# The end of a two-block layer kernel: last gate quarter in two halves, the mean per token earlier, one factor computed on GpSimd

## The chip, the core and the metric

The kernel runs on one core of a Trainium2 chip. The metric is the device time of one execution in microseconds. Three runs of the kernel before gave 1013.49 us as the median (1012.62 to 1014.14).

## The reference

The reference sends 256 tokens of width 1024 through two transformer blocks (four kinds of token mixers, a gated convolutional feed-forward part, a short-convolution layer, and a differential attention layer). All arithmetic is float32. Only its last lines matter here: the per-layer embedding of the second layer, which is added to x and is the output.

```
def per_layer_embed(x, p_i, g_pre, w_gate, w_proj, g_post):
    gate = jax.nn.sigmoid(rms_norm_2(x, g_pre) @ w_gate)
    return rms_norm_2(gate * (p_i @ w_proj), g_post)
...
x = x + per_layer_embed(x, p[i], g_pre_ple[i], w_ple_gate[i], w_ple_proj[i], g_post_ple[i])
```

So the end computes: x normed by its mean square per token, times a 1024 x 1024 weight (the gate), a sigmoid, the product with a projection that is ready by then, the mean square of that product per token, a norm by it, a gain, and the addition of x.

## The kernel before

All weights pass through one stream of blocks of 128 x 2048 elements. Each block is loaded by a DMA into a ring of three slots, ScalarE makes its rounded high part (`w_hi`, line 1639), VectorE the low part (`w_lo`, line 2433), and TensorE multiplies three times (high by high, high by low, low by high) and sums in PSUM. Each engine has its own list of instructions, written out by hand in the order in which they run; semaphores tie the lists together. An engine works strictly down its list, so whatever stands behind a waiting instruction waits too.

The activations are held channel-major (8 chunks of 128 channels x 256 tokens) nearly everywhere. The last gate (`ple_gate1`, four weight blocks, numbered 0 to 3, in function `last_layer` of TensorE) is computed token-major instead. Its result is 256 tokens x 1024 columns, cut in four quarters b = 0 to 3: quarter b holds token tile b // 2 (128 tokens) and column half b % 2 (512 columns). Before, quarter b is summed in PSUM bank `LAST_GATE_BANK[b]`, that is banks 6, 0, 1 and 2.

The sum of the last feed-forward layer (`y`) lies in PSUM banks 0 to 3 when the gate starts. VectorE scales it out of these banks in `add_before_gate` with five instructions, which raise the semaphore `y_scaled` five times: bank 0 in two halves (line 3114), then banks 1, 2 and 3 (line 3112). The list of VectorE has these five not in a row: behind bank 2 come two low parts of x chunks (line 2446), two updates of x (line 3118), one half weight block (line 3101), two more low parts, and only then bank 3. TensorE waits for the bank it is about to write: for the third scaling before quarter 2, for the fourth before quarter 3.

`mean_by_token` sums the squares of x over the channels for each token, with the result in PSUM bank 4. ScalarE turns this into r = (mean + eps)^-0.5 (`rstd_x`, lines 1720 and 1727), loads the sigmoid table (line 2230), and starts with `last_products`. There, for each quarter, ScalarE takes the sigmoid out of PSUM (line 2264), VectorE multiplies by the projection (line 3378) and by the gain (line 3382), and ScalarE squares and sums (line 2268). When the two quarters of a token tile are squared, VectorE turns the first sum into a bias (line 3386), ScalarE loads the table for logarithm and exponential (line 2287) and computes the factor as exp(-0.5 ln(...)) (lines 2276, 2277). The result is z times factor plus x. For that x is turned token-major on TensorE (`turn_x`, 16 transposes at line 885, into the banks `TURN_BANK` = 4, 5, 3, 7), and VectorE does the four additions (line 3394). Each raises a semaphore at which SyncE stores 256 KB (line 506).

The code at its places, with line numbers:

Of the kernel before, what the change touches and what calls it, by code (L numbers as in the profile page):

```python
# [16 lines left out]
P = 128  # L17
# [92 lines left out]
SUMS_OF_ROW = [3, 3, 4, 4, 3, 4, 4, 4]  # L110
LED = (3, 5, 6)
SIX_FIRST = (6, 0, 1, 2, 3, 4, 5, 7)
SQUARES_OF_POST = [5, 5, 3, 5, 5, 5]
SUMS_OF_POST = [2, 2, 0, 2, 2, 2]
# [3 lines left out]
TURN_BANK = (4, 5, 3, 7)  # L118
# [7 lines left out]
def build(nc, weights, small_in, x_in, masks_in, ident_in, channel_in, row_in, w_gk_in, p_in, table_in,  # L126
# [4 lines left out]
    with ExitStack() as ctx:  # L131
        sems = {}

        def sem(name):
            if name not in sems:
                sems[name] = ctx.enter_context(nc.semaphore(name))
            return sems[name]
# [304 lines left out]
        sum_of_squares, norm_bias, norm_r = (att_stat[0][:, a:b] for a, b in ((0, 4), (4, 6), (6, 8)))  # L442
# [108 lines left out]

# [3 lines left out]
        def _(pe):  # L555
# [246 lines left out]
            def last_layer(p, q):  # L802
# [27 lines left out]

                def part(j, b, k, a, w, first=False):

                    t, half = divmod(b, 2)
                    at = k % 2 * D + half * 512
                    return add(PS[:, LAST_GATE_BANK[b], :], a[:, k, t * P:(t + 1) * P], w[:, (n + j) % RING, at:at + 512], first)
# [13 lines left out]
                for b in (2, 3):  # L849
                    pe.wait_ge(sem("y_scaled"), T_PARTS * q + b + 1)  # L850
                    high(0, b, 0, True)
                    high(0, b, 1)
# [43 lines left out]
                gate(3, 0).then_inc(bank_summed, 1)  # L896
                gate(3, 1).then_inc(bank_summed, 1)
                mean_by_token()
                gate(3, 2).then_inc(bank_summed, 1)
                pe.wait_ge(sem("x_rstd"), p + 2)  # L900
                pe.wait_ge(sem("proj_copied"), 6)
                for b in range(4):
                    turn_x(b)
                gate(2, 3)
                gate(3, 3).then_inc(bank_summed, 1)
# [716 lines left out]
        def _(act):  # L1622
# [633 lines left out]
            def last_products(q):  # L2256
# [8 lines left out]

                def square(b):
                    act.wait_ge(sem("ple_product"), 5 + b + 1)
                    act.activation(sq4[:, b, :], by_quarter[:, b, :], ACT.Square, accum_out=sum_of_squares[:, b:b + 1]) \  # L2268
                        .then_inc(sem("y_squares"), 1)

                def rstd(t):

                    act.wait_ge(sem("y_squares"), y_square(q, 2 * t + 2))
                    act.wait_ge(sem("y_sum"), y_sum(q, t + 1))
                    r = norm_r[:, t:t + 1]
                    link(act.activation(r, sum_of_squares[:, 2 * t + 1:2 * t + 2], ACT.Ln, scale=1.0 / D, bias=norm_bias[:, t:t + 1]))
                    act.activation(r, r, ACT.Exp, scale=-0.5).then_inc(sem("y_rstd"), 1)
# [4 lines left out]
                square(0)  # L2282
                square(1)
                gate_sigmoid(2)
                square(2)
                gate_sigmoid(3)
                act.preload_act_table_set(TABLES)
                rstd(0)
                square(3)
                rstd(1)  # L2290
# [118 lines left out]
        def _(dve):  # L2409
# [961 lines left out]
            def last_products(z, q):  # L3371
# [7 lines left out]

                def gain(b):  # L3380
# [3 lines left out]
                def bias(t):  # L3384
                    dve.wait_ge(sem("y_squares"), y_square(q, 2 * t + 1))
                    ts(norm_bias[:, t:t + 1], sum_of_squares[:, 2 * t:2 * t + 1], 1.0 / D, EPS, ALU.mult, ALU.add) \
                        .then_inc(sem("y_sum"), 1)

                def result(b):
                    if b % 2 == 0:  # L3390
                        settle()
                        dve.wait_ge(sem("y_rstd"), q + b // 2 + 1)
                        dve.wait_ge(sem("mixed_turned"), 4 + 4)
# [290 lines left out]
```

## Time and profile before

| | |
|---|---|
| median of 3 runs | 1013.49 us |
| the profiled execution | 1012.54 us, of which the span of the profile is 1010.8 us |
| TensorE matmul busy | 996.4 us (99%), 8338 instructions |
| VectorE busy | 845.2 us (84%) |
| ScalarE busy | 622.3 us (62%) |
| GpSimd busy | 7.3 us (1%) |
| share of the chain that ended last | PE 93%, DVE 2%, ACT 2%, DMA 2% |

TensorE works nearly without a break from the start to about 1002 us of the span. Only the last 9 us belong to others: the last products on ScalarE and VectorE in turn, and the stores. In the last of the 40 slices of the page the busy share of PE is 6 tenths, and DVE and ACT show 6 tenths each. In the rows PE is TensorE, PEld its weight load, DVE VectorE, ACT ScalarE, POOL GpSimd, SP SyncE.

### The profile page before, as it was taken

To read this page: it belongs to the slowest core of one execution; us is meant where nothing else is said; L and a number is where in the kernel's file an instruction comes from. 1 tells how busy PE (TensorE), PEld (TensorE's weight loads), DVE (VectorE), ACT (ScalarE), POOL (GpSimd) and SP (SyncE) were. 2 spreads that over 40 slices of the span, in tenths; PEclk is the share of its full clock that TensorE was granted. 3 is DMA by queue.
4 is the path that set the end of the run, shared out by engine and by line. 5 is a ranking of instruction groups with operands and counts; after the bars stand their busy time and mean duration, and the time that the engine had idled before them with its cause. 6 is when DMAs were issued, how large, how long until landed. Compare 5 with 4: busy or idle time off the path is not lost.

```text
span 1010.8 us, 20806 instructions
## 1 busy us (share of the span) xinstructions
PE 996.4 (99%) x8338; PEld 934.7 (92%) x8338; DVE 845.2 (84%) x1216; ACT 622.3 (62%) x858; POOL 7.3 (1%) x18
## 2 busy tenths in 40 slices
PE   8999999999999999999999999999999999999996
PEld 7999999999999998899999999989999999999985
DVE  6974896899988878879998888889776899988886
ACT  6754565657565655467575646775677666565665
POOL 0000001000000000000000000000000000000000
PEclk9999999999999999999999999999999999999998
DMA  9533315555655545656556555535444356655531
GB/s 333 182 117 97 126 49 196 168 205 172 209 203 172 202 144 190 206 211 233 197 187 207 190 184 197 175 128 179 156 149 166 128 184 207 212 197 177 202 126 42
DMA packets 26786, 177.04 MB, mean 175 GB/s; under 512 B 3261, under 2 KB 3541, under 8 KB 6368
## 3 DMA queue, kind: packets, MB, share of 16 engines
q1 hardware_dynamic: 25616, 171.31, 48.9%
q0 software_dynamic: 1104, 4.78, 1.6%
q8 instruction: 50, 0.82, 0.4%
q14 instruction: 16, 0.13, 0.0%
HBM read 175.02 MB, written 2.63 MB: 176 GB/s over the span
## 4 chain that ended last, share of the span: by engine, by line
PE 93%; DVE 2%; ACT 2%; DMA 2%; issue 0%; SPq 0%; DVEq 0%
PE PS L606 80%; PE PS L557 12%; DMA arena<-masks_in 1%; DVE arena L2574 1%; DMA raw<-weights 0%; DVE w_lo L2433 0%; PE PS L1544 0%; ACT xn L2268 0%; ACT arena L1807 0%; ACT w_hi L1639 0%; ACT arena L2264 0%; PE PS L912 0%; ACT arena L2003 0%; ACT arena L1808 0%; DVE arena L2984 0%
## 5 line engine op out<-in xcount | busy, mean ns | idle before, releaser
L606 PE MATMUL PS<-h_store,w_hi 128*128 128x256 f32 (+1 forms) x1840 | 475.9, 338 | 2.0 <-DVE w_lo L2488 1.6
L2433 DVE TENSOR_TENSOR w_lo<-raw,w_hi 128x2048 fp32r<-128x2048 f32 x152 | 347.9, 2290 | 50.5 <-ACT w_hi L1639 45.4
L606 PE MATMUL PS<-h_store,w_lo 128*128 128x256 f32 (+1 forms) x1400 | 365.4, 281 | 0.1
L1639 ACT ACTIVATE w_hi<-raw 128x2048 fp32r<-128x2048 f32 x155 | 296.1, 1911 | 82.6 <-PE PS L606 69.5
L606 PEld LDWEIGHTS PS<-h_store,w_hi 128*128 128x128 f32 x1840 | 303.8, 187 | 41.3 <-DVE w_lo L2488 2.0
L606 PEld LDWEIGHTS PS<-h_store,w_lo 128*128 128x128 f32 (+1 forms) x1400 | 253.2, 188 | 0.5 <-DVE h_store L3047 0.3
L606 PE MATMUL PS<-act_hi,w_hi 128*128 128x256 f32 x688 | 191.0, 279 | 0.1
L606 PE MATMUL PS<-act_hi,w_lo 128*128 128x256 f32 x688 | 190.6, 279 | 0.1
L606 PE MATMUL PS<-act_lo,w_hi 128*128 128x256 f32 x688 | 187.5, 279 | 0.0
L606 PEld LDWEIGHTS PS<-act_hi,w_hi 128*128 128x128 f32 x688 | 129.3, 188 | 1.6 <-DVE act_hi L3047 0.6
L606 PEld LDWEIGHTS PS<-act_hi,w_lo 128*128 128x128 f32 x688 | 129.3, 188 | 0.3 <-DVE act_hi L3047 0.3
L606 PEld LDWEIGHTS PS<-act_lo,w_hi 128*128 128x128 f32 x688 | 127.4, 188 | 0.0
L2116 ACT ACTIVATE arena<-PS 128x512 f32<-128x512 f32 x51 | 30.2, 593 | 88.6 <-PE PS L606 88.6
L2108 ACT ACTIVATE arena<-arena,channel 128x256 f32<-128x256 f32 x132 | 63.6, 531 | 13.4 <-DVE arena L3187 12.2
L606 PE MATMUL PS<-w_hi,h_store 128*128 128x256 f32 (+1 forms) x352 | 70.6, 306 | 0.5 <-ACT h_store L1763 0.5
L3164 DVE SCALAR_TENSOR_TENSOR arena<-arena,channel 128x254 f32<-128x254 f32 x132 | 57.9, 480 | 7.6 <-DVE arena L3160 0.3
L3160 DVE SCALAR_TENSOR_TENSOR arena<-arena,channel 128x255 f32<-128x255 f32 x132 | 57.7, 479 | 0.9 <-ACT arena L2108 0.9
L606 PEld LDWEIGHTS PS<-w_hi,h_store 128*128 128x128 f32 x352 | 54.6, 188 | 3.9 <-ACT w_hi L1753 0.9
L3185 DVE TENSOR_TENSOR arena<-PS,arena 128x512 f32<-128x512 f32 x51 | 35.0, 686 | 21.1 <-ACT arena L2116 21.1
L606 PE MATMUL PS<-w_lo,h_store 128*128 128x256 f32 (+1 forms) x176 | 45.1, 302 | 0.5 <-DVE w_lo L2433 0.5
L557 PE MATMUL PS<-h_store,w_hi 128*128 128x256 f32 x256 | 45.4, 279 | 0.0
L557 PE MATMUL PS<-arena 64*64 64x64 f32 (+8 forms) x1356 | 41.5, 224 | 0.0
(385 smaller groups left out, 1138.1 us busy)
## 6 DMA issues: line engine op xcount, KB each, us to landing
raw<-weights SPq DMA_DIRECT2D x155, 1024.0 KB, 5.0
raw<-weights SPq DMA_DIRECT2D x12, 256.0 KB, 4.0
arena<-masks_in SPq DMA_DIRECT2D x1, 1600.0 KB, 12.2
bias_by_key<-bias_by_distance POOLq DMA_DIRECT2D x1, 1536.0 KB, 8.1
x<-x_in SPq DMA_DIRECT2D x4, 256.0 KB, 4.3
raw<-weights SPq DMA_DIRECT2D x2, 512.0 KB, 8.9
arena<-weights POOLq DMA_DIRECT2D x2, 512.0 KB, 6.0
arena<-bias_by_key POOLq DMA_DIRECT2D x1, 1024.0 KB, 6.4
```

Of the source, the lines that this page charges most:

```text
L557: return pe.matmul(o, lhs, rhs, start=start, stop=stop)
L606: return pe.matmul(o, lhs, rhs, start=start, stop=stop, skip_group_check=True)
L1639: act.activation(w_hi[:, slot, :], raw[:, slot, :], ACT.Copy).then_inc(hi_ready, 1)
L2108: ins = act.activation(dst[:, c, :], src[:, c, :], ACT.Identity, scale=w, bias=b)
L2116: act.activation(low, PS[:, bank:bank + 2, TOK:512], ACT.Copy).then_inc(sem("low_copied"), 1)
L2433: tt(w_lo[:, slot, :], raw[:, slot, :], w_hi[:, slot, :].bitcast(F), ALU.subtract).then_inc(lo_ready, 1)
L2574: mark(stt(dst, PS[:, bank_of_block(n), f * TOK:(f + 1) * TOK - d], ch("gdn_conv", (3 - d) * 6 + 2 * s + f), dst, ALU.mult, ALU.add))
L3160: stt(y[:, c, 1:TOK], src[:, c, 0:TOK - 1], channel[:, bass.ds(col(1) + c, 1)], y[:, c, 1:TOK], ALU.mult, ALU.add).then_inc(ready[0], 1)
L3164: ins = stt(y[:, c, 2:TOK], src[:, c, 0:TOK - 2], channel[:, bass.ds(col(0) + c, 1)], y[:, c, 2:TOK], ALU.mult, ALU.add)
L3185: tt(z, PS[:, bank:bank + 2, 0:TOK], low, ALU.add).then_inc(sem("parts_added"), 1)
```

## The change

Five things change, all in the last few dozen microseconds:

1. Quarter 3 of the gate is summed as two halves of 256 columns, the first in bank 2 and the second in bank 3. Every 512-column matmul of this quarter becomes two of 256 columns, and its last two blocks are now run half after half, at the very end. Before its first matmul TensorE waits for the fifth scaling as well, since bank 3 is now written.
2. `mean_by_token` stands behind quarter 0 of the last block, before it stood behind quarter 1.
3. The transposes of quarter 2 go to bank 6, before to bank 3. So they wait for the first sigmoid, which reads bank 6.
4. The factor of the first token tile is computed as a power on GpSimd, in place of the logarithm and exponential on ScalarE. Ahead of the power (line 553 of the changed file) the program has one more GpSimd instruction of the kind ISA on the same line, which has no operands and no wait. The sum of both squares and eps is formed by one VectorE instruction, and the squares carry the factor 1/1024 themselves.
5. The last square is done on VectorE as one multiply-and-sum of 256 columns; ScalarE squares the first half of quarter 3 only, and loads its table behind the last sigmoid as before. The first result is added before the last half products, the other three at the end.

The diff, cut to its core:

```diff
-SQUARES_OF_POST = [5, 5, 3, 5, 5, 5]
-SUMS_OF_POST = [2, 2, 0, 2, 2, 2]
+SQUARES_OF_POST = [5, 5, 3, 5, 5, 4]
+SUMS_OF_POST = [2, 2, 0, 2, 2, 3]
...
-TURN_BANK = (4, 5, 3, 7)
+TURN_BANK = (4, 5, 6, 7)
...
+            link(pool.memset(minus_half, -0.5))
+            pool.wait_ge(sem("y_sum"), y_sum(5, 1))
+            pool.tensor_tensor(norm_r[:, 0:1], norm_bias[:, 0:1], minus_half, ALU.pow).then_inc(sem("first_rate"), 1)
...
+                def last_quarter(j, k, half, a, w, first=False, final=False):
+
+                    at = k % 2 * D + 512 + half * TOK
+                    return add(PS[:, 2 + half, 0:TOK], a[:, k, P:TOK], w[:, (n + j) % RING, at:at + TOK], first, final)
+
                 def part(j, b, k, a, w, first=False):
 
+                    if b == 3:
+                        last_quarter(j, k, 0, a, w, first)
+                        return last_quarter(j, k, 1, a, w, first)
...
                 for b in (2, 3):
                     pe.wait_ge(sem("y_scaled"), T_PARTS * q + b + 1)
+                    if b == 3:
+                        pe.wait_ge(sem("y_scaled"), T_PARTS * q + 5)
                     high(0, b, 0, True)
                     high(0, b, 1)
...
                 gate(3, 0).then_inc(bank_summed, 1)
+                mean_by_token()
                 gate(3, 1).then_inc(bank_summed, 1)
-                mean_by_token()
                 gate(3, 2).then_inc(bank_summed, 1)
                 pe.wait_ge(sem("x_rstd"), p + 2)
                 pe.wait_ge(sem("proj_copied"), 6)
+                pe.wait_ge(sem("gate_sigmoid"), 5 + 1)
                 for b in range(4):
                     turn_x(b)
-                gate(2, 3)
-                gate(3, 3).then_inc(bank_summed, 1)
+                for half in range(2):
+                    for k in range(4, KC):
+                        last_quarter(k // 2, k, half, a_hi, w_hi)
+                        last_quarter(k // 2, k, half, a_lo, w_hi)
+                        last = last_quarter(k // 2, k, half, a_hi, w_lo, False, k == KC - 1)
+                    last.then_inc(bank_summed, 1)
...
                 gate_sigmoid(0)
                 gate_sigmoid(1)
                 square(0)
+                gate_sigmoid(2)
                 square(1)
-                gate_sigmoid(2)
                 square(2)
-                gate_sigmoid(3)
+                half_sigmoid(0)
+                act.wait_ge(sem("ple_product"), 5 + 4)
+                act.activation(sq4[:, 3, 0:TOK], prod[:, 6, :], ACT.Square, scale=D ** -0.5, accum_out=sum_of_squares[:, 3:4]) \
+                    .then_inc(sem("y_squares"), 1)
+                half_sigmoid(1)
                 act.preload_act_table_set(TABLES)
-                rstd(0)
-                square(3)
-                rstd(1)
+                act.wait_ge(sem("y_sum"), y_sum(q, 3))
+                r = norm_r[:, 1:2]
+                link(act.activation(r, sum_of_squares[:, 4:5], ACT.Ln, bias=norm_bias[:, 1:2]))
+                act.activation(r, r, ACT.Exp, scale=-0.5).then_inc(sem("y_rstd"), 1)
...
                 product(0)
                 product(1)
                 gain(0)
-                bias(0)
                 gain(1)
                 product(2)
+                mean(0, 0, 1, 2)
                 gain(2)
-                bias(1)
-                product(3)
-                gain(3)
-                for b in range(4):
-                    result(b)
+                half_product(0)
+                dve.wait_ge(sem("first_rate"), 1)
+                result(0)
+                half_gain(0)
+                half_product(1)
+                dve.wait_ge(sem("ple_product"), 5 + 5)
+                v = prod[:, 7, :]
+                dve.tensor_tensor_reduce(sq4[:, 3, TOK:512], v, v, 1.0 / D, 0.0, ALU.mult, ALU.add, sum_of_squares[:, 4:5]) \
+                    .then_inc(sem("y_sum"), 1)
+                mean(1, 2, 3, 4)
+                half_gain(1)
+                result(1)
+                dve.wait_ge(sem("y_rstd"), q + 1)
+                result(2)
+                result(3)
```

On TensorE, in the gate's first block (h_store holds the activations, w_hi and w_lo the weights), the rows from the last matmuls of quarter 2 over quarter 3 into the low parts were before:

```order
L606 MATMUL PS<-w_hi,h_store 128x512
L606 MATMUL PS<-w_lo,h_store 128x512
L606 MATMUL PS<-w_hi,h_store 128x512 [waits y_scaled]
L606 MATMUL PS<-w_lo,h_store 128x512
L606 MATMUL PS<-w_hi,h_store 128x512
L606 MATMUL PS<-w_lo,h_store 128x512
L606 MATMUL PS<-w_hi,h_store 128x512 [waits lo_chunk]
L606 MATMUL PS<-w_hi,h_store 128x512 x3
```

and are now:

```order
L608 MATMUL PS<-w_hi,h_store 128x512
L608 MATMUL PS<-w_lo,h_store 128x512
L608 MATMUL PS<-w_hi,h_store 128x256 [waits y_scaled]
L608 MATMUL PS<-w_hi,h_store 128x256
L608 MATMUL PS<-w_lo,h_store 128x256 x2
L608 MATMUL PS<-w_hi,h_store 128x256 x2
L608 MATMUL PS<-w_lo,h_store 128x256 x2
L608 MATMUL PS<-w_hi,h_store 128x512 [waits lo_chunk]
L608 MATMUL PS<-w_hi,h_store 128x512 x2
```

Quarter 3 is the group behind the last `waits y_scaled`. Its four wide matmuls are now eight narrow ones, and the count for which that wait holds is five scalings, before four.

On TensorE again, from quarter 1 of the last block to the transposes (`ones,arena` is the mean per token, `ident,x` the transposes), the rows were before:

```order
L606 MATMUL PS<-w_hi,h_store 128x512 x2
L606 MATMUL PS<-w_lo,h_store 128x512
L606 MATMUL PS<-w_hi,h_store 128x512 x2
L606 MATMUL PS<-w_lo,h_store 128x512
L606 MATMUL PS<-ones,arena 128x2 [waits x_sum]
L606 MATMUL PS<-ones,arena 128x2
L606 MATMUL PS<-w_hi,h_store 128x512 x2
L606 MATMUL PS<-w_lo,h_store 128x512
L606 MATMUL PS<-w_hi,h_store 128x512 x2
L606 MATMUL PS<-w_lo,h_store 128x512
L885 MATMUL PS<-ident,x 128x128 [waits proj_copied,x_rstd]
```

and are now:

```order
L608 MATMUL PS<-w_hi,h_store 128x512 x2
L608 MATMUL PS<-w_lo,h_store 128x512
L608 MATMUL PS<-ones,arena 128x2 [waits x_sum]
L608 MATMUL PS<-ones,arena 128x2
L608 MATMUL PS<-w_hi,h_store 128x512 x2
L608 MATMUL PS<-w_lo,h_store 128x512
L608 MATMUL PS<-w_hi,h_store 128x512 x2
L608 MATMUL PS<-w_lo,h_store 128x512
L608 MATMUL PS<-w_hi,h_store 128x512 x2
L608 MATMUL PS<-w_lo,h_store 128x512
L608 MATMUL PS<-w_hi,h_store 128x512 x2
L608 MATMUL PS<-w_lo,h_store 128x512
L897 MATMUL PS<-ident,x 128x128 [waits gate_sigmoid,proj_copied,x_rstd]
```

The mean stands six matmuls sooner, and the first transpose has a third wait.

On VectorE, the end of the list (products at line 3378, gains at 3382, results at 3394; the line numbers of the changed file are 3397 and 3401 for products, 3405 and 3409 for gains, 3420 for results) was before:

```order
L3386 TENSOR_SCALAR arena<-arena 128x1 [waits y_squares]
L3382 TENSOR_TENSOR arena<-arena 128x512 [waits ple_product]
L3378 TENSOR_TENSOR arena<-arena 128x512 [waits gate_sigmoid]
L3382 TENSOR_TENSOR arena<-arena 128x512 [waits ple_product]
L3386 TENSOR_SCALAR arena<-arena 128x1 [waits y_squares]
L3378 TENSOR_TENSOR arena<-arena 128x512 [waits gate_sigmoid]
L3382 TENSOR_TENSOR arena<-arena 128x512 [waits ple_product]
L3394 SCALAR_TENSOR_TENSOR arena<-arena,PS 128x512 [waits mixed_turned,y_rstd,dve_own]
L3394 SCALAR_TENSOR_TENSOR arena<-arena,PS 128x512
L3394 SCALAR_TENSOR_TENSOR arena<-arena,PS 128x512 [waits mixed_turned,y_rstd,dve_own]
L3394 SCALAR_TENSOR_TENSOR arena<-arena,PS 128x512
```

and is now:

```order
L3414 TENSOR_SCALAR arena<-arena 128x1 [waits y_squares]
L3405 TENSOR_TENSOR arena<-arena 128x512 [waits ple_product]
L3401 TENSOR_TENSOR arena<-arena 128x256 [waits gate_sigmoid]
L3420 SCALAR_TENSOR_TENSOR arena<-arena,PS 128x512 [waits mixed_turned,dve_own,first_rate]
L3409 TENSOR_TENSOR arena<-arena 128x256 [waits ple_product]
L3401 TENSOR_TENSOR arena<-arena 128x256 [waits gate_sigmoid]
L3439 ISA xn,arena<-arena 128x256 [waits ple_product]
L3439 ISA arena 128x1
L3414 TENSOR_SCALAR arena<-arena 128x1 [waits y_squares]
L3409 TENSOR_TENSOR arena<-arena 128x256 [waits ple_product]
L3420 SCALAR_TENSOR_TENSOR arena<-arena,PS 128x512 [waits mixed_turned,dve_own]
L3420 SCALAR_TENSOR_TENSOR arena<-arena,PS 128x512 [waits mixed_turned,dve_own,y_rstd]
```

One result now stands behind `first_rate`, GpSimd's semaphore, ahead of the last half product, and the multiply-and-sum (line 3439) stands between the last product and the second mean.

## Rows read from the trace of the kernel before

**Rows 1.** PE timeline, gate's first block; start us, us, engine line op, count.

```profile
977.91 0.47 PE L606 MATMUL PS<-w_hi,h_store 128*128 128x512 f32 x1 [0.53 <-ACT h_store L1763]
...
980.52 0.39 PE L606 MATMUL PS<-w_lo,h_store 128*128 128x512 f32 x1
980.75 0.39 PE L606 MATMUL PS<-w_hi,h_store 128*128 128x512 f32 x1
```

**Rows 2.** VectorE timeline of the same stretch.

```profile
978.00 1.28 DVE L3112 TENSOR_TENSOR arena<-PS,arena 128x512 f32<-128x512 f32 x2
...
980.78 1.22 DVE L3101 TENSOR_TENSOR w_lo<-raw,w_hi 128x1024 fp32r<-128x1024 f32 x1
...
982.71 0.68 DVE L3112 TENSOR_TENSOR arena<-PS,arena 128x512 f32<-128x512 f32 x1
```

**Rows 3.** chain that ended last, up to 996 us; start us, us, what.

```profile
977.78 0.14 issue
977.91 18.19 PE PS L606 x81
```

**Rows 4.** PE timeline from the mean per token to the end.

```profile
995.71 0.50 PE L606 MATMUL PS<-ones,arena 128*128 128x2 f32 x4
996.07 0.71 PE L606 MATMUL PS<-w_hi,h_store 128*128 128x512 f32 x2
...
997.53 1.91 PE L885 MATMUL PS<-ident,x 128*128 128x128 f32 x16
999.19 0.71 PE L606 MATMUL PS<-w_hi,h_store 128*128 128x512 f32 x2
...
1001.80 0.39 PE L606 MATMUL PS<-w_lo,h_store 128*128 128x512 f32 x1
```

**Rows 5.** ScalarE timeline of the end.

```profile
996.25 0.26 ACT L1720 ACTIVATE arena<-PS,eps 128x4 f32<-128x4 f32 x1 [6.25 <-PE PS L606]
...
998.06 1.27 ACT L2264 ACTIVATE arena<-PS,arena 128x512 f32<-128x512 f32 x2
999.61 0.63 ACT L2268 ACTIVATE xn<-arena 128x512 f32<-128x512 f32 x1 [0.28 <-DVE arena L3378]
...
1003.60 1.28 ACT L2287 ACT_TABLE_LOAD   x1
```

**Rows 6.** VectorE timeline of the end.

```profile
993.32 0.43 DVE L2465 TENSOR_TENSOR arena<-arena 128x256 f32<-128x256 f32 x1
998.88 1.29 DVE L3378 TENSOR_TENSOR arena<-arena 128x512 f32<-128x512 f32 x2 [5.13 <-ACT arena L2264]
...
1005.51 2.72 DVE L3394 SCALAR_TENSOR_TENSOR arena<-arena,PS 128x512 f32<-128x512 f32 x4 [0.48 <-ACT arena L2277]
```

**Rows 7.** chain that ended last, its last piece.

```profile
1007.57 0.66 DVE arena L3394
```

**Rows 8.** PE timeline, 256-column matmuls in steady run.

```profile
968.94 0.28 PE L606 MATMUL PS<-act_hi,w_hi 128*128 128x256 f32 x1
969.05 0.28 PE L606 MATMUL PS<-act_lo,w_hi 128*128 128x256 f32 x1
```

**Rows 9.** ScalarE timeline, one reading of 256 columns of PSUM.

```profile
969.62 0.36 ACT L1788 ACTIVATE xn<-PS 128x256 f32<-128x256 f32 x1
```

**Rows 10.** groups by form, VectorE; line, op, shapes, count, busy us, mean ns.

```profile
L3454 DVE CUSTOM_DVE_ANT_0 arena<-PS,arena 128x256 f32<-128x256 f32 x16 | 6.7, 420 | 0.0
...
L3454 DVE DVE_READ_ACCUMULATOR2_ANT arena<- 128x1 f32 x16 | 1.3, 83 | 0.0
```

**Rows 11.** groups on GpSimd, its largest memset.

```profile
L522 POOL MEMSET zeros_r<- 128x512 f32 x1 | 0.5, 530 | 0.0
```

**Rows 12.** windows; us, busy of PE, PEld, DVE, ACT, POOL, then PEclk.

```profile
1004.00:1005.00 1.00, 0.00 (x0) 0.00 (x0) 0.97 (x2) 0.99 (x2) 0.00 (x0) 0.89 0.00 0
1005.00:1006.00 1.00, 0.00 (x0) 0.00 (x0) 0.52 (x2) 0.97 (x4) 0.00 (x0) 0.50 0.00 0
```

**Rows 13.** groups by form, PE, first 7 us: the zero matmuls.

```profile
L606 PE MATMUL PS<-zeros_r 128*128 128x512 f32 x13 | 4.7, 531 | 1.5 <-POOL zeros_r L522 1.5
```

More of the change, by code:

```diff
@@ L109 @@
 }
-SUMS_OF_ROW = [3, 3, 4, 4, 3, 4, 4, 4]
+SUMS_OF_ROW = [3, 3, 4, 4, 3, 4, 4, 5]
 LED = (3, 5, 6)
 SIX_FIRST = (6, 0, 1, 2, 3, 4, 5, 7)
-SQUARES_OF_POST = [5, 5, 3, 5, 5, 5]
-SUMS_OF_POST = [2, 2, 0, 2, 2, 2]
+SQUARES_OF_POST = [5, 5, 3, 5, 5, 4]
+SUMS_OF_POST = [2, 2, 0, 2, 2, 3]
 POST_BANK = (5, 4, 4, 5, 4)
@@ L441, in build @@
         by_quarter = prod.rearrange("p c n -> p (c n)").rearrange("p (b n) -> p b n", b=4)
-        sum_of_squares, norm_bias, norm_r = (att_stat[0][:, a:b] for a, b in ((0, 4), (4, 6), (6, 8)))
+        sum_of_squares, norm_bias, norm_r, minus_half = (att_stat[0][:, a:b] for a, b in ((0, 5), (5, 7), (7, 9), (9, 10)))
         def hi_at(p, c):
@@ L2264, in gate_sigmoid, with half_sigmoid @@
                     act.activation(flat(z[b]), PS[:, LAST_GATE_BANK[b], :], ACT.Sigmoid, scale=r_x[:, at:at + 1]).then_inc(sem("gate_sigmoid"), 1)
+                def half_sigmoid(half):
+                    act.wait_ge(bank_summed, bank_sum(7, 4 + half))
+                    act.activation(z[3][:, half, :], PS[:, 2 + half, 0:TOK], ACT.Sigmoid, scale=r_x[:, TOK + 2:TOK + 3]) \
+                        .then_inc(sem("gate_sigmoid"), 1)
                 def square(b):
                     act.wait_ge(sem("ple_product"), 5 + b + 1)
-                    act.activation(sq4[:, b, :], by_quarter[:, b, :], ACT.Square, accum_out=sum_of_squares[:, b:b + 1]) \
+                    act.activation(sq4[:, b, :], by_quarter[:, b, :], ACT.Square, scale=D ** -0.5, accum_out=sum_of_squares[:, b:b + 1]) \
                         .then_inc(sem("y_squares"), 1)
[L2271 to L2277, printed above, removed]
                 act.wait_ge(sem("x_rstd"), 8)
@@ L3378, in product, with half_product @@
                     tt(by_quarter[:, b, :], quarter(z[b]), by_quarter[:, b, :], ALU.mult).then_inc(sem("ple_product"), 1)
+                def half_product(half):
+                    dve.wait_ge(sem("gate_sigmoid"), 5 + 4 + half)
+                    tt(prod[:, 6 + half, :], z[3][:, half, :], prod[:, 6 + half, :], ALU.mult).then_inc(sem("ple_product"), 1)
                 def gain(b):
@@ L3382, in gain, with half_gain, mean @@
                     mark(tt(quarter(z[b]), by_quarter[:, b, :], gain_row[:, (b % 2) * 512:(b % 2 + 1) * 512], ALU.mult))
[L3384 to L3387, printed above, removed]
+                def half_gain(half):
+                    dve.wait_ge(sem("ple_product"), 5 + 4 + half)
+                    mark(tt(z[3][:, half, :], prod[:, 6 + half, :], gain_row[:, 512 + half * TOK:512 + (half + 1) * TOK], ALU.mult))
+                def mean(t, first, second, squares):
+                    dve.wait_ge(sem("y_squares"), y_square(q, squares))
+                    ts(norm_bias[:, t:t + 1], sum_of_squares[:, first:first + 1], sum_of_squares[:, second:second + 1], EPS,
+                       ALU.add, ALU.add).then_inc(sem("y_sum"), 1)
                 def result(b):
[L3390 to L3393, printed above, removed]
+                    settle()
+                    dve.wait_ge(sem("mixed_turned"), 4 + 4)
                     stt(by_quarter[:, b, :], quarter(z[b]), norm_r[:, b // 2:b // 2 + 1], PS[:, TURN_BANK[b], :], ALU.mult, ALU.add) \
```

## The prediction

> **What bounds the kernel now.** I read the chain of waits first, then the timelines of TensorE, VectorE and ScalarE from 968 us on, then a few groups and the windows of the last microseconds. The chain has one piece of TensorE that starts at 977.91 us and runs 18.19 us through 81 matmuls [rows 3]: from the first matmul of the last gate to the mean per token TensorE never stops. So whatever holds TensorE up there moves the end by as much, and whatever is taken out in front of the mean comes off it. Behind the mean the chain goes to ScalarE and VectorE, which hand the quarters to each other: the reader is to see in the ScalarE and VectorE timelines that sigmoid, product, square and again product follow within 0.1 us of each other [rows 5, 6]. TensorE works beside them until its last matmul at 1001.80 [rows 4], and it is no longer what they wait for. The last addition on VectorE ends at 1008.23 (1007.57 plus 0.66) [rows 7], and the stores behind it, 2.6 us to the end of the span at 1010.8, are the same in both kernels.
>
> **The change part by part.**
>
> First, the new wait in the gate's first block. Quarter 3 starts there at 980.75 now [rows 1]; the two scalings of banks 1 and 2 began at 978.00 and took 1.28 us together, so the old wait was over at 979.28 [rows 2] and cost nothing. The changed kernel writes bank 3 as well, and must wait for the fifth scaling. On VectorE that is the single L3112 that starts at 982.71 and lasts 0.68, so it ends at 983.39 [rows 2]; between it and the fourth stand the half weight block of 1.22 us at 980.78 [rows 2] and seven smaller instructions, none of which waits for TensorE, so it comes no sooner. TensorE starts a matmul 0.14 us after its release [rows 3]: 983.53 in place of 980.75, that is 2.78 us of standing still. The first matmul after a wait lasts 0.47 us where the next ones last 0.39 [rows 1], which adds 0.08. Nothing gives this back: TensorE has no idle time from there to the mean [rows 3], and its in-order list holds all the rest of the gate behind the wait. ScalarE's high part of the last weight block, which waits for the first block to be used, slips with it, but it and VectorE's low part come some 2 us before they are wanted.
>
> Second, twelve matmuls of 512 columns in the first two blocks become 24 of 256. A steady 512-column matmul costs 0.226 us: from 996.07 to 997.53 there are 6 and some hundredths of start-up, and (1001.80 - 999.19)/11 is 0.237 with a start-up of 0.1 in it [rows 4]. A 256-column one costs 0.11 to 0.12 [rows 8]; I take 0.117. 24 times 0.117 less 12 times 0.226 is 0.10 us. Bounds: 0.11 would give -0.07, 0.12 gives +0.17. With the stall the shift is 2.78 + 0.08 + 0.10 = 2.96 us.
>
> Third, the mean stands 6 matmuls sooner: 6 times 0.226 = 1.36 us off. It starts at 995.71 now [rows 4], so at 995.71 + 2.96 - 1.36 = 997.31. It needs the sum of squares, whose last fold ends at 993.75 now [rows 6]. That fold stands behind work that the stall pushes by up to 2.5 us, which makes about 996.2, still a microsecond early.
>
> Fourth, the walk from the mean's start to the last addition, which takes 12.52 us now (995.71 to 1008.23). Taken from the start of the mean as zero: the first sigmoid starts at 2.35 (998.06) and the first product at 3.17 (998.88) [rows 5, 6], and the first square 0.73 after its product (999.61) [rows 5]. These steps are the same after. Then ScalarE: a square holds it for 0.63 [rows 5], so the third sigmoid, now ahead of the second square, starts at 4.53 and ends by 5.2. VectorE: products and gains of 512 columns follow each other at 0.61 (a pair takes 1.29, one 0.69 by the difference of ends) [rows 6]: second product 3.78, gains 4.39 and 5.00, third product 5.61, first mean 6.22, third gain 6.29. The third square follows the third product by 0.73 at 6.34 and ends at 6.97. The first half sigmoid reads 256 columns in 0.36 [rows 9], and its product starts at 7.38. Then the chain lies on VectorE: product half 0.35, first result at 7.73 with 0.66 (four results take 2.72) [rows 6], gain half 0.35 at 8.39, second half product at 8.74. Its sigmoid stands behind the half square (7.84) and is done by 8.7. The multiply-and-sum must see that product written, which makes 9.20; it takes 0.42 and 0.08 for its sum, by the 16 such instructions of 256 columns in the attention [rows 10]. Second mean 9.70, gain half 9.77, then the wait for that gain's write, and the results at 10.23, 10.89, 11.55, end at 12.29. ScalarE loads its table for 1.28 us [rows 5] from 8.54 to 9.82, and needs 0.5 more for logarithm and exponential, so the second factor is there at 10.35, before it is wanted at 10.89. This walk is 0.23 us shorter than now. Bounds: each of its eight hand-overs between engines or through a semaphore may be 0.05 off either way, so 0.2 less to 0.6 us more (a late hand-over adds, an early one is often covered by the other engine).
>
> The stretch of TensorE beside it is not in the way. The mean takes 0.36 (995.71 to 996.07), two quarters 2.71, so the transposes start at 3.1 from the mean, and the added wait, for the first sigmoid, ends at 3.05. The transposes take 1.66 us (997.53 to 999.19) [rows 4] and a half 12 times 0.117 = 1.4: the first half is summed at 6.5 against 6.97, when ScalarE comes to it, the second at 7.9 against 8.3. Without the split TensorE would finish at the same time, so the two halves buy only that the first can be read earlier.
>
> The power on GpSimd is new: no row shows one. It starts when the first mean is written, at 6.37, and its answer is wanted at 7.73, so it has 1.36 us. The nearest rows are a GpSimd memset of 512 columns at 0.53 us [rows 11] and, as an upper bound, ScalarE's load of a table together with such a memset, 1.81 us. I take 0.6, nearest to GpSimd's own row, and it is hidden; from 1.36 on every tenth counts in full, since VectorE stands at that wait with the last half product behind it. The upper bound gives +0.45.
>
> Sum: 2.96 - 1.36 - 0.23 = +1.37 us. The profiled execution took 1012.54 us, its span 1010.8; the span would be 1012.2 and that execution 1013.9. The median lies 0.95 above the profiled one, so I put the sum on the median: 1013.49 + 1.37, rounded to 1014.8 us. The change takes a quarter of a gate block out of the path and pays two of them for it at bank 3.
>
> **The rivals.**
>
> Rival A, TensorE's clock falls in the stall (slower). At the end of the run TensorE's last matmul starts at 1001.80 and ends at 1002.19 [rows 4], and the granted clock is at 0.89 in the window from 1004 and at 0.50 in the next [rows 12], so it fell at about 1004.8, 2.6 us after the last matmul. The new stall leaves TensorE without work for about as long: from 980.91 to 983.53 is 2.6 us. If the clock falls from 2.4 to 1.2 GHz there, the gate's matmuls go on at half pace until it rises. What that costs can be read from the start: the 13 matmuls on zeros take 4.7 us, mean 531 ns [rows 13], where 12 times 0.226 plus 0.39 would be 3.1. That is 1.6 us lost in one such rise, so 1014.8 + 1.6 = 1016.4 us, and 1018 if it lasts twice as long. Against it: the two times are only just alike, and TensorE was busy in front of the stall. The Trainium skill (TensorE: Matmul & The Clock Gate, Part 1) says that the gate is set by how busy TensorE has recently been and is not in step with the kernel's start; by that rule some executions would show this and others not, which no run here can tell yet.
>
> Rival B, GpSimd answers late. For it speaks the nameless extra instruction ahead of the power, against it that it stands ahead of the wait, so that it can be done long before the power is released. By the bound above 1014.8 + 0.45 = 1015.3 us. The Trainium skill (GPSIMD Engine Reference, 2.1 Instruction dispatch) says that the first call of a newly loaded GpSimd routine pays about 6 us without an instruction in the profile; an estimate by that page, 5.95 + 0.53 - 1.36 = 5.1 more, would be 1019.9 us. No row here shows it.
>
> Rival C, the stall is not there: the fifth scaling comes in time, or VectorE gets to it earlier. Then the 2.86 are gone and the sum is 0.10 - 1.36 - 0.23 = -1.49, or 1012.0 us. The rows of VectorE speak against it, since nothing of its list ahead of 982.71 changes. It stays for what I may have misread of the tail: a shorter tail by over a microsecond would look the same.
>
> **How the numbers follow.** Forecast 0.60, rival A 0.20, rival B 0.08, rival C 0.12. The forecast's own range is 1014.2 to 1015.6 (0.2 less to 0.6 more in the tail, 0.17 from the split, a tenth or two from the measurement). What a measurement of this kernel can tell from no change is 0.2%, 2.03 us, so the lines are 1011.5 and 1015.5. Slower: all of A, 0.20, half of B, 0.04, a tenth of the forecast, 0.06, together 0.30. Faster: a quarter of C, 0.03. Same: 0.67. The range reaches down to take in the centre of C, 1011.8, and up through A's single rise, 1017.4; outside are B by the page's figure, A twice as long and C's far side, less than 2 in 10.
>
> **What would show it.** The stall: an idle time of 2.6 to 2.8 us on TensorE in front of the first 256-column matmul of the last gate, released by L3131 of the changed file (the scaling). If that is under 0.5 us, the forecast is wrong by its largest term. The mean: six 512-column matmuls between it and quarter 1's end, and start at 997.3. The tail: 12.3 us from the mean to the last addition. GpSimd: one power of under 1.3 us, and no idle time in front of the first result at L3420. Clock: granted 1.00 in every window of the gate; 0.5 in any of them is rival A.

## The result, and the profile after

| | before | after |
|---|---|---|
| median of 17 runs each | 1013.42 us | 1016.06 us |
| lowest and highest | 1012.29, 1014.84 | 1013.58, 1017.36 |
| profiled execution, its span | 1012.54, 1010.8 | 1016.03, 1014.2 |

The ratio is 1.0026 with a 95% interval of 1.0020 to 1.0033: the change makes the kernel slower by 2.6 us. My sum was 1.4 us slower, and its own range, 1014.2 to 1015.6, ends below the measured median.

The timeline of TensorE in the gate's first block (start us, us, engine, line, op, count), which answers to [rows 1], shows the new wait:

```profile
978.54 0.47 PE L608 MATMUL PS<-w_hi,h_store 128*128 128x512 f32 x1 [0.53 <-ACT h_store L1780]
...
981.16 0.39 PE L608 MATMUL PS<-w_lo,h_store 128*128 128x512 f32 x1
984.17 0.77 PE L608 MATMUL PS<-w_hi,h_store 128*128 128x256 f32 x2 [2.62 <-DVE arena L3131]
984.74 0.63 PE L608 MATMUL PS<-w_lo,h_store 128*128 128x256 f32 x2
985.16 0.63 PE L608 MATMUL PS<-w_hi,h_store 128*128 128x256 f32 x2
```

The next matmul was due at 981.39 and starts at 984.17, 2.78 us later, as worked out. It is also slow: two matmuls of 256 columns take 0.63 us from the start of the first to the end of the second, where the last ones of the same kernel take 0.40, and pairs follow each other at 0.42 where 0.24 is the steady pace at its end. The windows (us, busy times of PE, PEld, DVE, ACT, POOL, then PEclk) say why:

```profile
983.00:984.00 1.00, 0.00 (x0) 0.00 (x0) 1.00 (x4) 0.00 (x0) 0.00 (x0) 0.96 0.00 0
984.00:985.00 1.00, 0.83 (x4) 0.86 (x5) 1.00 (x4) 0.00 (x0) 0.00 (x0) 0.50 0.00 0
985.00:986.00 1.00, 1.00 (x6) 1.00 (x6) 1.00 (x1) 0.00 (x0) 0.00 (x0) 0.50 0.00 0
986.00:988.00 2.00, 2.00 (x9) 1.65 (x8) 1.01 (x1) 0.00 (x0) 0.00 (x0) 0.67 0.00 0
988.00:990.00 2.00, 2.00 (x12) 1.72 (x11) 0.00 (x0) 1.26 (x1) 0.00 (x0) 1.00 0.00 0
```

The granted clock falls to 0.50, that is 1.2 GHz, at the end of the stall (0.96 in the window from 983) and is back at about 987.3 (0.67 over two microseconds is 0.5 for 1.3 of them). From 984.17 to 987.3 TensorE works at about half pace, which loses up to half of 3.16 us, 1.6 us. Measured from the restart to the mean per token it is a little less: 15.34 us here (984.17 to 999.51), where the two kernels below that have the stall and keep their clock take 13.93 and 13.94.

The chain that ended last (start us, us, what) had TensorE without a break for 18.19 us from the gate's first matmul on [rows 3]. Now it runs over VectorE up to the fifth scaling and comes to TensorE only behind the stall:

```profile
978.71 1.20 DVE arena L3131 x2
979.91 0.79 DVE h_store L2465 x2
980.70 0.79 DVE x L3137 x2
981.49 1.13 DVE w_lo L3120
982.63 0.79 DVE h_store L2465 x2
983.42 0.61 DVE arena L3131
984.03 0.14 issue
984.17 15.86 PE PS L608 x76
```

The reader is to see the last three scalings (L3131 twice, in one row, then seven other instructions in four rows, then L3131 alone) and TensorE behind the last. The end of VectorE's timeline answers to [rows 6], and GpSimd's only row in it is the power:

```profile
1005.70 0.21 DVE L3414 TENSOR_SCALAR arena<-arena 128x1 f32<-128x1 f32 x1
1005.83 0.69 DVE L3405 TENSOR_TENSOR arena<-arena 128x512 f32<-128x512 f32 x1
1006.94 0.42 DVE L3401 TENSOR_TENSOR arena<-arena 128x256 f32<-128x256 f32 x1 [0.43 <-ACT arena L2285]
1007.28 0.74 DVE L3420 SCALAR_TENSOR_TENSOR arena<-arena,PS 128x512 f32<-128x512 f32 x1
...
1008.76 0.42 DVE L3439 CUSTOM_DVE_ANT_0 xn<-arena 128x256 f32<-128x256 f32 x1
1009.11 0.08 DVE L3439 DVE_READ_ACCUMULATOR2_ANT arena<- 128x1 f32 x1
...
1009.69 2.06 DVE L3420 SCALAR_TENSOR_TENSOR arena<-arena,PS 128x512 f32<-128x512 f32 x3
```

```profile
1006.06 0.89 POOL L553 TENSOR_TENSOR arena<-arena 128x1 f32<-128x1 f32 x1 [234.48 <-DVE arena L3414]
```

The power is done at 1006.95, and the first result behind it starts at 1007.28 without a wait. The mean started at 999.51 and the last addition ends at 1011.76: a tail of 12.25 us, where my walk had 12.29 and the kernel before 12.52. The first transpose starts at 1002.70 without a wait, so the new wait for the first sigmoid costs nothing here.

### The profile page after: what moved, and what is told of

It reads as the page before. It is cut to its first block, busy times and chain, and to the rows that moved or that the text cites. A ratio compares the mean times of both kernels' runs of the same rounds, so it can differ in the third digit from the quotient of the medians.

```text
span 1014.2 us, 20863 instructions
## 1 busy us (share of the span) xinstructions
PE 999.6 (99%) x8362; PEld 937.9 (92%) x8362; DVE 845.4 (83%) x1220; ACT 621.5 (61%) x857; POOL 8.4 (1%) x20
## 4 chain that ended last, share of the span: by engine, by line
PE 93%; DVE 3%; ACT 2%; issue 1%; DMA 1%; SPq 0%; DVEq 0%
PE PS L608 80%; PE PS L559 12%; DVE w_lo L2452 1%; DMA raw<-weights 1%; DVE arena L2593 1%; ACT w_hi L1656 0%; PE PS L1561 0%; DVE x L3137 0%; DVE h_store L2465 0%; ACT arena L1824 0%; DVE arena L3397 0%; DVE arena L3131 0%; PE PS L929 0%; ACT arena L2020 0%; ACT arena L1825 0%
## 5 line engine op out<-in xcount | busy, mean ns | idle before, releaser
L608 PEld LDWEIGHTS PS<-w_hi,h_store 128*128 128x128 f32 x368 | 57.1, 191 | 6.5 <-DVE arena L3131 3.0
```

Source lines behind the costliest of these rows:

```text
L608: return pe.matmul(o, lhs, rhs, start=start, stop=stop, skip_group_check=True)
```

## The experiments

Ratios are against the kernel before on the same chip. Its medians there were 1012.82 us (first four experiments), 1013.02 (next four) and 1013.15 (last two). "The kernel before", "the changed kernel" and "the kernel with the half later" (the fourth experiment) are the three that the others start from. Single runs of one kernel spread over 1 to 4 us, so medians that differ by a few tenths are not told apart; what the profiles say of such differences stands in a table behind the experiments.

**The wait alone.** The kernel before with the new wait and nothing else:

```diff
                 for b in (2, 3):
                     pe.wait_ge(sem("y_scaled"), T_PARTS * q + b + 1)
+                    if b == 3:
+                        pe.wait_ge(sem("y_scaled"), T_PARTS * q + 5)
```

> The kernel before with one line more: in front of quarter 3 of the gate's first block TensorE waits for the fifth scaling too, as the changed kernel does; nothing else is changed. Theory: this wait alone costs the stall of 2.8 us, and in the executions where the granted clock falls in it another 1.4 to 1.7 us, so the median is 3 to 4.3 us above before (1016.5 to 1017.7) and single runs lie between +2.7 and +4.7. Rival: the stall is given back by the chain behind it (TensorE is not the bound there) and the loss of the changed kernel comes from its tail; then this kernel stays within 1 us of before.

Measured: 1016.73 us (1015.34 to 1018.68, 5 runs), ratio 1.0039 (1.0026 to 1.0053), 3.9 us slower. The stall is on TensorE's row again:

```profile
983.21 0.57 PE L606 MATMUL PS<-w_hi,h_store 128*128 128x512 f32 x1 [2.64 <-DVE arena L3114]
```

and the granted clock is 0.71 in the window from 983, and 0.50 in those from 984 and 985. Nothing is given back: the mean starts 22.29 us behind the gate's first matmul, 4.49 more than before, and the tail behind it is 12.53 us as before (12.52). The rival that blames the tail falls.

**The stall kept, TensorE kept busy in it.** The changed kernel with eleven matmuls whose result nobody reads:

```diff
                     if b == 3:
+                        for _ in range(11):
+                            add(PS[:, 4, :], a_hi[:, 0, P:TOK], w_hi[:, n % RING, 0:512], True, True)
                         pe.wait_ge(sem("y_scaled"), T_PARTS * q + 5)
```

> The changed kernel with 11 matmuls of 512 columns into the unused PSUM bank 4 at the place where TensorE waits for the fifth scaling; their result is overwritten later and never read. They take 2.5 of the 2.8 us of the stall, so the stall stays and TensorE is not idle in it. Theory: the granted clock stays at 1.00, and the kernel takes what my sum gave, before + 1.4 (1014.4 to 1015.2), that is 1 to 1.6 us less than the changed kernel. Rival: the clock has no part in the median, and it takes the same as the changed kernel (1016) or more.

Measured: 1014.29 us (1013.81 to 1015.48, 11 runs), ratio 1.0014 (1.0005 to 1.0023), 1.5 us slower than before. The granted clock is 1.00 in each window of this stretch:

```profile
983.00:984.00 1.00, 0.97 (x5) 0.51 (x4) 1.00 (x3) 0.00 (x0) 0.00 (x0) 1.00 0.00 0
984.00:985.00 1.00, 1.00 (x9) 1.00 (x10) 1.00 (x3) 0.00 (x0) 0.00 (x0) 1.00 0.00 0
```

This kernel does eleven matmuls more than the changed one and is faster than it. It is the kernel that my sum described (+1.37), and its difference to the changed one, 1.2 us by the two medians' distances from before, is the clock. (The changed one is measured again beside the kernel before in the last experiment.)

**The fifth scaling earlier.** In the changed kernel, VectorE of the last layer does `scale(3)` straight behind `scale(2)`:

```diff
                 scale(2)
+                if u == 7 - 1:
+                    scale(3)
                 chunk_lo(u + 1, 0)
...
                 chunk_lo(u + 1, 3)
-                scale(3)
+                if u != 7 - 1:
+                    scale(3)
```

> The changed kernel, but in the last layer VectorE does the fifth scaling straight behind the fourth. Bank 3 is free at about 979.9 in place of 983.4, so the wait of TensorE at quarter 3 ends before it is reached. Theory: no stall, no fall of the clock, and the gain of the earlier mean and the shorter tail is left: before - 1.5 (1011.5 to 1012.4). Price: the low parts of chunks 0 to 3 and the half weight block come 0.6 us later on VectorE, of which at most 0.3 us reaches TensorE. Rival (the tail costs what was lost): 1014 or more.

Measured: 1011.56 us (1010.70 to 1012.33, 11 runs), ratio 0.9983 (0.9974 to 0.9992), 1.3 us faster than before. TensorE's chain is one piece again:

```profile
979.14 17.19 PE PS L608 x88
```

**The half in bank 3 later.** VectorE stays as it is; TensorE does the second half of quarter 3 behind the first high products of the second block (the edit cut to its core):

```diff
-                for b in (2, 3):
-                    pe.wait_ge(sem("y_scaled"), T_PARTS * q + b + 1)
-                    if b == 3:
-                        pe.wait_ge(sem("y_scaled"), T_PARTS * q + 5)
-                    high(0, b, 0, True)
-                    high(0, b, 1)
...
+                high_of_next(2)
+                pe.wait_ge(sem("y_scaled"), T_PARTS * q + 5)
+                for k in range(2):
+                    last_quarter(0, k, 1, a_hi, w_hi, k == 0)
+                    last_quarter(0, k, 1, a_hi, w_lo)
+                    last = last_quarter(0, k, 1, a_lo, w_hi)
+                last.then_inc(block_used, 1)
```

> The changed kernel with VectorE as it is, but TensorE does the second half of quarter 3 (bank 3) later: all its matmuls of the first block stand behind the first four high products of the second block, where the fifth scaling is done. Theory: no stall, so as with the early scaling, before - 1.5 (1011.5 to 1012.4); the first block's slot comes free 0.6 us later, which has room. If the high part of the last weight block becomes late by this, the mean waits for the sum of squares and it is up to 0.6 us worse. Rival: 1014 or more.

Measured: 1011.55 us (1010.89 to 1012.04, 11 runs), ratio 0.9986 (0.9977 to 0.9995), 1.3 us faster. Two different ways to take the wait away give the same time. From the gate's first matmul (978.35) to the mean (995.02) it is 16.67 us; before it was 17.80. The move of six matmuls should give 17.80 - 1.36 = 16.44, so the split of the quarter costs 0.23 us, where I had 0.10 and a bound of 0.17. The kernel with the earlier scaling gives 0.24 in the same way (16.68), so it is not this kernel's own order.

**The mean alone.** The kernel before with the mean moved, and nothing else:

```diff
                 gate(3, 0).then_inc(bank_summed, 1)
+                mean_by_token()
                 gate(3, 1).then_inc(bank_summed, 1)
-                mean_by_token()
```

> The kernel before with the mean per token one gate quarter sooner, nothing else. My sum took the full 1.36 us for this move. Theory: that is only to be had together with the halves, since here the last quarter is one piece that TensorE still finishes at the same time (last matmul started at 1001.80); its sigmoid, which started at 1002.91, can come at most to about 1002.25, so before - 0.65. Rival: the whole 1.36 us come off, because the chain behind the mean alone sets the end.

Measured: 1012.28 us (1010.90 to 1013.91, 11 runs), ratio 0.9994 (0.9985 to 1.0003): 0.7 us less by the medians, in an interval that takes in no change. The profile decides. The mean starts 16.44 us behind the gate's first matmul, the full 1.36 sooner, but the tail behind it is 13.21 us, 0.69 longer, so 0.67 us is left. The last sigmoid waits for TensorE now, which it did not before:

```profile
1001.26 0.69 ACT L2264 ACTIVATE arena<-PS,arena 128x512 f32<-128x512 f32 x1 [0.58 <-PE PS L606]
```

**The mean put back.** The kernel with the half later:

```diff
                 gate(3, 0).then_inc(bank_summed, 1)
-                mean_by_token()
                 gate(3, 1).then_inc(bank_summed, 1)
+                mean_by_token()
```

> The kernel in which the half of bank 3 is done later (no stall), with the mean put back behind quarter 1 of the last block. Theory (my sum): the mean is worth 1.36 us, so that kernel + 1.36, which is before + 0.1 (1012.7 to 1013.3). Rival: the gain without the stall comes from the halves and the power, and the mean's place is worth under 0.5 us.

Measured: 1013.01 us (1012.21 to 1014.05, 11 runs), ratio 0.9997 (0.9988 to 1.0006), no change against before; 1.3 us is what the mean's place is worth beside the halves (-0.01 against -1.27 us). TensorE stands idle for 1.21 us in front of the transposes here, at the wait for the first sigmoid, and the tail is 12.23 us all the same, so that wait does not reach the end. Halves, power and square on VectorE together shorten the tail by 0.29 us and the split costs 0.21, so together they are worth about nothing; none of the three was tried alone.

**Two powers.** The kernel with the half later:

```diff
+            link(pool.tensor_tensor(norm_r[:, 0:1], norm_bias[:, 0:1], minus_half, ALU.pow))
             pool.tensor_tensor(norm_r[:, 0:1], norm_bias[:, 0:1], minus_half, ALU.pow).then_inc(sem("first_rate"), 1)
```

> The kernel in which the half of bank 3 is done later, with the power on GpSimd done twice, one behind the other. One took 0.89 us in the profile of the changed kernel and ended at 1006.95, while the result that needs it started at 1007.28, so 0.3 us are spare. Theory: the second adds 0.9 to 1.0 us, 0.3 of it is hidden, and VectorE's in-order list passes on the rest: + 0.6 to 0.7 us (1012.1 to 1012.3). Rival: VectorE has room behind that wait and the time does not change by more than 0.2.

Measured: 1012.51 us (1011.88 to 1013.58, 11 runs), ratio 0.9992 (0.9983 to 1.0001), 0.8 us more than with one power (-0.51 against -1.27). The second took 0.74 us, and VectorE waited for it:

```profile
1003.27 0.75 DVE L3435 SCALAR_TENSOR_TENSOR arena<-arena,PS 128x512 f32<-128x512 f32 x1 [0.44 <-POOL arena L554]
```

The row shows 0.44 us of it as a wait, and from the gate's first matmul to the last addition this profile is 0.50 us longer than with one power; the medians say 0.8, and the difference is of the size of their error.

**The mean in the middle of the quarter.** The kernel with the half later; quarter 0 of the last block runs chunk by chunk with the mean between:

```diff
-                gate(3, 0).then_inc(bank_summed, 1)
-                mean_by_token()
+                for k in (6, 7):
+                    part(3, 0, k, a_hi, w_hi)
+                    part(3, 0, k, a_lo, w_hi)
+                    last = part(3, 0, k, a_hi, w_lo)
+                    if k == 6:
+                        mean_by_token()
+                last.then_inc(bank_summed, 1)
```

> The kernel in which the half of bank 3 is done later, with the mean half a quarter sooner still, between the two chunks of quarter 0 of the last block: three matmuls, 0.68 us. The sum of squares is ready about then, which may cost some tenths, and TensorE's halves leave 0.4 us before they become the bound. Theory: - 0.2 to - 0.5 us against that kernel (1011.1 to 1011.4). Rival: TensorE waits for the sum of squares and the halves come too late, no gain or up to 0.3 us lost.

Measured: 1011.87 us (1011.55 to 1012.65, 11 runs), ratio 0.9989 (0.9980 to 0.9998): no better than with the mean behind quarter 0, by the distances from before (-1.15 against -1.27), which the medians cannot tell apart; the profile is 0.44 us longer in the stretch. TensorE now waits for the sum of squares, and the first half sigmoid waits for TensorE:

```profile
994.62 0.61 PE L608 MATMUL PS<-ones,arena 128*128 128x2 f32 x4 [0.44 <-DVE arena L2503]
```

```profile
1002.00 0.47 ACT L2304 ACTIVATE arena<-PS,arena 128x256 f32<-128x256 f32 x1 [0.25 <-PE PS L608]
```

The mean starts only 0.07 us sooner (16.60 us behind the gate's first matmul, against 16.67), and the tail is 0.51 us longer (12.77 against 12.26). My theory fell here, and its rival holds in both its parts.

**A shorter idle time.** The changed kernel with 4 in place of 11 matmuls in the stall:

> The changed kernel with 4 in place of 11 matmuls into the unused bank at the wait: the stall stays at 2.8 us, but TensorE stands idle for only about 1.7 us of it (2.6 in the changed kernel, 0.1 with 11). Theory: what costs the 1.5 us above the stall is the fall of the granted clock, and it falls only where TensorE is idle long enough; then this kernel lies near the one kept busy (before + 1.4 to 1.9). Rival: a shorter idle time only makes the fall less frequent or not at all less so, and the median stays at before + 2.6 or so.

Measured: 1014.55 us (1013.53 to 1016.27, 12 runs), ratio 1.0015 (1.0006 to 1.0023), 1.4 us slower than before, as with eleven, and 1.4 us less than the changed kernel beside it (next). TensorE was idle for 1.64 us and the granted clock stayed at 1.00:

```profile
985.00 0.51 PE L608 MATMUL PS<-w_hi,h_store 128*128 128x256 f32 x2 [1.64 <-DVE arena L3133]
```

```profile
984.00:985.00 1.00, 0.00 (x0) 0.00 (x0) 1.00 (x3) 0.00 (x0) 0.00 (x0) 1.00 0.00 0
985.00:986.00 1.00, 0.99 (x8) 1.00 (x9) 1.00 (x3) 0.00 (x0) 0.00 (x0) 1.00 0.00 0
```

**The changed kernel again**, beside it on the same chip:

> The changed kernel once more, unchanged, on the same chip as the kernel with the shorter idle time. Theory: before + 2.6 to 3.2, with single runs spread over 2 to 3 us, and the granted clock at 0.5 behind the stall in the profile. Rival (the earlier runs were a matter of their chip): before + 1.4.

Measured: 1015.97 us (1014.38 to 1016.56, 11 runs), ratio 1.0024 (1.0015 to 1.0033), 2.8 us slower. The loss is there again, so it is not a matter of one session. In this profile the clock fell after TensorE had resumed:

```profile
983.98 0.48 PE L608 MATMUL PS<-w_hi,h_store 128*128 128x256 f32 x2 [2.65 <-DVE arena L3131]
```

```profile
984.00:985.00 1.00, 1.00 (x8) 1.00 (x9) 1.00 (x3) 0.00 (x0) 0.00 (x0) 1.00 0.00 0
985.00:986.00 1.00, 1.00 (x5) 0.80 (x4) 1.00 (x1) 0.00 (x0) 0.00 (x0) 0.58 0.00 0
```

From the restart to the mean it takes 15.44 us (983.98 to 999.42), against 13.94 in the kernel with the shorter idle time.

**One stretch in all profiles.** The gate's first matmul starts anywhere from 976.95 to 979.48 us in these profiles, though the edits lie behind it, but for one memset of 128x1 on GpSimd; 0.6 us of the 3.4 by which the two spans of the result differ arise there. So the profiles are best compared from that matmul on. The table gives the microseconds from it to the mean's start, from there to the end of the last addition, and the sum against before:

| kernel | to the mean | tail | against before |
|---|---|---|---|
| before | 17.80 | 12.52 | |
| changed | 20.97 | 12.25 | +2.90 |
| changed, again | 21.06 | 12.24 | +2.98 |
| the wait alone | 22.29 | 12.53 | +4.50 |
| kept busy | 19.46 | 12.24 | +1.38 |
| shorter idle time | 19.46 | 12.25 | +1.39 |
| scaling earlier | 16.68 | 12.23 | -1.41 |
| half later | 16.67 | 12.26 | -1.39 |
| the mean alone | 16.44 | 13.21 | -0.67 |
| mean put back | 18.01 | 12.23 | -0.08 |
| two powers | 16.67 | 12.76 | -0.89 |
| mean in the quarter | 16.60 | 12.77 | -0.95 |

Each row is one execution, and kernels with the same tail agree in it within 0.03 us.

## Why the prediction was right in its direction, and short by half

The direction held, and so did nearly each step; what failed is the chance given to the clock. The measured 1016.06 us is not what the sum gave. It lies beyond the sum's own range, and beyond 1015.5, the line above which I had put only 0.30; it is near the time of rival A, 1016.4. The wide range held it only because it had been drawn out to take in that rival.

1. The stall. 2.78 us was worked out, and 2.78 us it is; the 0.14 us from the scaling's end to the matmul held as well. The step read two lists against each other: which bank a quarter writes, and where in VectorE's list that bank comes free. The kernel with the wait alone shows that nothing gives it back.
2. The split. 0.10 us was worked out, with 0.17 as the bound, and it measures 0.21 to 0.24 in the kernels that have the split and no stall (scaling earlier, half later, mean put back). The 256-column matmuls at the end of the changed kernel follow each other at 0.12 us, which makes the 0.17; where the rest lies stays open.
3. The mean. 1.36 us was worked out; 1.3 us lie between the two kernels that differ in it alone, by the medians and in the table. But I treated it as standing by itself, and it does not: without the halves it gives 0.7 us, for then the last sigmoid waits for TensorE. What I wrote of the halves, that they only let the first be read earlier, named the very thing that makes the move pay.
4. The tail. 12.29 us against 12.25. The order of its pieces held too: the first result was not kept waiting, and the last three ran back to back. On VectorE no step of the walk is off by more than 0.1 us. ScalarE's last table load starts 0.24 us later than worked out, and its factor still comes some 0.2 us before it is wanted.
5. The power. I took 0.6 us and it takes 0.89; the bounds (0.53 to 1.81) held it. It started 0.15 us after the first mean's end. With 0.33 us to spare it is hidden, and a second one is not. Rival B did not happen: the result behind the power does not wait. The 6 us that the Trainium skill (GPSIMD Engine Reference, 2.1 Instruction dispatch) gives for a first call of a newly loaded routine do not show at the power, whose row starts 0.15 us after its release; whether they were spent earlier, at the instruction ahead of it, no row tells.
6. The clock. This is where the forecast failed. It set against rival A that "the two times are only just alike, and TensorE was busy in front of the stall", and gave it 0.20. The granted clock falls in all three profiles that have a stall of 2.6 us idle (the changed kernel twice, the wait alone once), and the gate's stretch of all the others is at 1.00. The kernel kept busy in the stall came out at before + 1.5 and the one with the shorter idle time at + 1.4, which is my sum; the changed kernel at + 2.6 and + 2.8. So rival A was the likelier case. The comparison on which I weighed it was looser than it looked: the time from the last matmul to the fall at the end of a trace, 2.6 us before, is 2.1 us in the kernel kept busy, 3.7 in the changed one and 5.1 in the changed one again, so one such row cannot say on which side a stall of 2.6 us lies. The price of rival A nearly held: 1.6 us was worked out, 1.4 and 1.5 us is what the two profiles of the changed kernel lose from the restart to the mean, and 1.2 to 1.4 lie between the medians. That the price came so near has some luck in it: the windows of the start, which the prediction does not show, give a granted clock of 1.00 for the 13 matmuls on zeros, so the 1.6 rested on the length of their rows alone.
   The fall is not in every execution. The mean granted clock of each run is on record, to three digits. It is 0.998 or 0.999 in all 33 runs of the kernel kept busy and of the two without the stall. In the changed kernel it is 0.997 or less in 14 of 17 runs and in 8 of the 11 later ones, with medians of 1016.3 and 1016.0 us; the six others, among them the lowest, 1013.58, have 0.998 or 0.999 and medians of 1015.1 and 1015.0. The three profiled runs with the fall have 0.996 and 0.997. (Only kernels with the changed tail are compared so. The kernel before has 0.996 to 0.998 with no fall in the gate, since its clock falls earlier before the end.) Of the twelve runs with the shorter idle time one has 0.997. No traces of the other runs were kept, so that the six are runs without the fall is argued and not shown. The Trainium skill (TensorE: Matmul & The Clock Gate, Part 1) has the gate not in step with the kernel's start. The three profiles agree: the clock fell 2.4 us (changed), 2.9 us (wait alone) and 3.8 us (changed, again) after the end of the last matmul in front of the stall, once before TensorE resumed, once 0.2 us and once 1.2 us behind it.
7. Rival C, the kernel without the stall, was worked out as 1.49 us faster; the two kernels that take the stall away are 1.3 us faster by the medians and 1.4 in the table.

Both halves in one bank would have needed no wait either. It was not tried. ScalarE would then read the first half while TensorE writes the second into the same bank, and no run here shows what comes of that.

## What to carry to other kernels

When a result is given another buffer, look up in the other engine's list when that buffer comes free, and not only how many buffers there are: here the wait for one more bank cost 2.8 us, twice what the earlier mean won, and one scaling moved up in VectorE's list turned 2.6 us lost into 1.3 us won. A stall on TensorE has a second price when the granted clock falls in it or behind it. The time from the last matmul to the fall at the end of the trace of the kernel before, 2.6 us, gave the warning: where a new stall is about as long, reckon with the fall. It is no sharp line, since the same time lies between 2.1 and 5.1 us at the ends of these traces. A step that is moved ahead is worth only what the next thing in line leaves of it: the mean alone gave half of its 1.36 us, with the halves all of it.

## What the runs showed of the hardware

The granted clock fell after TensorE had stood idle for 2.6 us between dense matmuls, in three profiles of three, and did not in one profile with 1.64 us idle and one with 1.21 (the mean put back, in front of the transposes). Behind the last matmul of a run it fell after 2.1 to 5.1 us, in four traces. In one of the three it fell only about 1.2 us after the matmuls had resumed, at 985.16 us where they had resumed at 983.98. It stayed at 1.2 GHz for 3.4 us in each of the three (983.9 to 987.3 in the changed kernel). Eleven matmuls of 512 columns whose result nobody reads kept it at 1.00 through the stall in one profile, and four did in another. A power of 128x1 elements on GpSimd takes 0.89 us, and a second one right behind it 0.74 us.
